# A hybrid decoder trunk on one core: the last feed-forward block and the start of the next layer reordered tile by tile

## What is computed

```python
h = rmsnorm(x, g_pre_mix) * (1 + sc1) + sh1
proj = h @ w_in                  # q, k, v, gates and indexer, 7240 columns
mixed = sigmoid(ga) * moba_attention(...) + sigmoid(gb) * dsa_attention(...)
x = x + gt1 * rmsnorm(mixed @ w_out, g_post_mix)

h = rmsnorm(x, g_pre_ffn) * (1 + sc2) + sh2
f = (silu(h @ w_gate) * (h @ w_up)) @ w_down      # 2816 wide
x = x + gt2 * rmsnorm(f, g_post_ffn)
```

## Time and profile before

| | |
|---|---|
| time, median of 3 runs | 891.76 us (891.47 to 892.01) |
| time of the profiled execution | 891.98 us |
| its span, first to last instruction | 890.1 us |
| TensorE busy with matmuls | 867.8 us, 97% |
| VectorE busy | 660.2 us, 74% |
| ScalarE busy | 411.6 us, 46% |
| GpSimd busy | 133.0 us, 15% |
| mean granted TensorE clock | 0.997 |

### The profile page before, as it was taken

The page is one execution under the profiler, slowest core; times in us unless marked ns, Lnnn a source line. Parts: engine busy times, 40 slices in busy tenths (PEclk is TensorE's granted clock), DMA queues, the critical chain, the costliest instruction groups (busy, mean ns, idle before and its releaser), DMA issues.

```text
span 890.1 us, 11600 instructions
## 1 busy us (share of the span) xinstructions
PE 867.8 (97%) x4241; PEld 713.6 (80%) x4241; DVE 660.2 (74%) x1090; ACT 411.6 (46%) x607; POOL 133.0 (15%) x164
## 2 busy tenths in 40 slices
PE   7999999999999999999999999999999999999996
PEld 5787788888877788888878778888888788888885
DVE  3778999887878767667568899988787865654842
ACT  1264654655636354344336555555564534434421
POOL 6500300200312030110232030020031200000302
PEclk9999999999999999999999999999999999999998
DMA  9787665567442977676634756566744274564611
GB/s 333 298 300 299 214 243 207 216 237 256 143 166 72 361 276 292 246 289 251 235 142 146 292 223 237 214 236 237 244 158 166 73 302 170 219 260 182 209 52 47
DMA packets 35577, 194.61 MB, mean 219 GB/s; under 512 B 4544, under 2 KB 4544, under 8 KB 19008
## 3 DMA queue, kind: packets, MB, share of 16 engines
q1 hardware_dynamic: 33984, 189.62, 57.8%
q0 software_dynamic: 1536, 4.24, 1.5%
HBM read 192.80 MB, written 1.05 MB: 218 GB/s over the span
## 4 chain that ended last, share of the span: by engine, by line
PE 80%; issue 9%; DVE 8%; DMA 2%; POOL 1%; ACT 1%; SPq 0%; DVEq 0%; POOLq 0%; ACTq 0%
PE ps L1142 23%; PE ps L1144 23%; PE ps L1143 23%; PE ps L1196 4%; PE ps L1248 1%; PE ps L1296 1%; DMA raw<-w_ada 1%; DVE pj L983 1%; DVE ffn_m L848 1%; PE ps L1276 1%; DVE x L1006 1%; DVE pj L968 1%; PE ps L1269 1%; PE ps L1268 1%; PE ps L1247 1%
## 5 line engine op out<-in xcount | busy, mean ns | idle before, releaser
L803 DVE TENSOR_TENSOR w_lo<-raw,w_hi 128x2048 fp32r<-128x2048 f32 (+1 forms) x132 | 302.2, 2298 | 52.2 <-ACT w_hi L581 50.3
L1142 PE MATMUL ps<-w_hi,t_hi 128*128 128x512 f32 (+2 forms) x832 | 325.3, 391 | 2.3 <-DVE t_lo L951 1.6
L1144 PE MATMUL ps<-w_hi,t_lo 128*128 128x512 f32 (+2 forms) x832 | 318.7, 383 | 0.0
L1143 PE MATMUL ps<-w_lo,t_hi 128*128 128x512 f32 (+2 forms) x832 | 318.1, 382 | 0.0
L581 ACT ACTIVATE w_hi<-raw 128x2048 fp32r<-128x2048 f32 (+1 forms) x132 | 249.8, 1896 | 25.4 <-DMA raw<-w_stream 16.0
L1142 PEld LDWEIGHTS ps<-w_hi,t_hi 128*128 128x128 f32 x832 | 156.3, 188 | 35.1 <-DVE t_lo L951 3.1
L1144 PEld LDWEIGHTS ps<-w_hi,t_lo 128*128 128x128 f32 x832 | 156.3, 188 | 30.9
L1143 PEld LDWEIGHTS ps<-w_lo,t_hi 128*128 128x128 f32 x832 | 156.5, 188 | 28.6
L1142 PE MATMUL ps<-w_hi,m_hi 128*128 128x512 f32 x240 | 99.6, 415 | 0.3
L1144 PE MATMUL ps<-w_hi,m_lo 128*128 128x512 f32 x240 | 94.3, 393 | 0.0
L1143 PE MATMUL ps<-w_lo,m_hi 128*128 128x512 f32 x240 | 93.7, 390 | 0.0
(11 more groups left out here) (170 smaller groups left out, 898.6 us busy)
## 6 DMA issues: line engine op xcount, KB each, us to landing
raw<-w_stream SPq DMA_DIRECT2D x128, 1024.0 KB, 5.9
ada<-w_ada SPq DMA_DIRECT2D x84, 512.0 KB, 5.0
raw<-w_ada SPq DMA_DIRECT2D x6, 512.0 KB, 11.8
raw<-w_stream SPq DMA_DIRECT2D x4, 656.0 KB, 8.6
scale_t<-gains POOLq DMA_DIRECT2D x4, 512.0 KB, 4.4
gate_t<-gains POOLq DMA_DIRECT2D x4, 512.0 KB, 5.1
pj<-w_ada SPq DMA_DIRECT2D x3, 512.0 KB, 16.1
mixed<-w_ada SPq DMA_DIRECT2D x2, 512.0 KB, 12.5
```

What stands on the lines that cost most here:

```text
L803: nc.vector.tensor_tensor(w_lo[:, U % RING, 0:n], raw[:, U % RAW, 0:n], w_hi[:, U % RING, 0:n].bitcast(F32), ALU.subtract).then_inc(s_lo, 1)
L1142: nc.tensor.matmul(dst, hi, w_h, start=first, stop=False)
L1143: nc.tensor.matmul(dst, hi, w_l, start=False, stop=False)
L1144: return nc.tensor.matmul(dst, lo, w_h, start=False, stop=last)
```

## The change

1. Block 10, the last of the feed-forward part, goes tile by tile on TensorE: up(10), down(9) with `turn_m` between its two banks, down(10), first for tile 0 and then for tile 1. ScalarE and VectorE get a `last_block` each, in which their part of block 10, the norm steps of the border and the splits of the next layer's units 1 to 4 are interleaved.
2. In layer 1 the first three chunks go tile by tile: chunks 0, 1 and 2 of tile 0, with the transposes of tile 1 after seven of the eight steps of chunk 2; then the three chunks of tile 1; then `turn_index`. The first index products move into chunk 3.
3. y is squared and gated in halves, one for each PSUM bank, and TensorE signals each bank. The two sums of a row are added in the first step of the inverse root.
4. VectorE makes all inverse roots of the feed-forward border, and behind the mixer all but that of y of tile 1. Its Newton steps are scalar_tensor_tensor instead of tensor_scalar.
5. h of tile 1 lies in hbuf 2 instead of hbuf 1, so that `copy_chunk` doesn't wait for the transposes of h; the squares' unused output goes to `mixed`.
6. 4 fills instead of 23 behind the feed-forward part.

The diff, cut to its core:

```diff
-MIXER_FILL, FFN_FILL, TURN_FILL = 16, 23, 4
+MIXER_FILL, FFN_FILL, TURN_FILL = 16, 4, 4
...
-OWN_NORMS = [n for n, (l, _, of, t) in enumerate(NORMS) if l >= 0 and of == "x"]
+OWN_NORMS = [n for n, (l, mid, of, t) in enumerate(NORMS)
+             if l >= 0 and (of == "x" or t == 0 or not mid)]
...
-            link(engine.tensor_scalar(u, ssq[:, t:t + 1], EPS, 0.5, ALU.add, ALU.mult))
+            if of == "y":
+                link(engine.tensor_scalar(u, ssq[:, t, 0:1], ssq[:, t, 1:2], EPS / 2, ALU.add, ALU.add))
+            else:
+                link(engine.tensor_scalar(u, ssq[:, t, 0:1], EPS / 2, None, ALU.add))
             link(engine.tensor_scalar(y.bitcast(I32), u.bitcast(I32), -0.5, RSQRT_BITS, ALU.mult, ALU.add))
             for step in range(NEWTON):
-                link(engine.tensor_scalar(e, y, u, y, ALU.mult, ALU.mult))
-                ins = engine.tensor_scalar(y, e, 1.5, y, ALU.subtract, ALU.mult)
+                if engine is nc.vector:
+                    link(engine.scalar_tensor_tensor(out=e, in0=y, scalar=u, in1=y, op0=ALU.mult, op1=ALU.mult))
+                    ins = engine.scalar_tensor_tensor(out=y, in0=e, scalar=1.5, in1=y, op0=ALU.subtract, op1=ALU.mult)
+                else:
+                    link(engine.tensor_scalar(e, y, u, y, ALU.mult, ALU.mult))
+                    ins = engine.tensor_scalar(y, e, 1.5, y, ALU.subtract, ALU.mult)
...
+                if of == "x":
+                    nc.scalar.activation(dst, x[:, t, :], ACT.Square, scale=(2.0 * D) ** -0.5,
+                                         accum_out=ssq[:, t, 0:1]).then_inc(s_sq, 1)
+                    return
+                for half in range(2):
+                    act.wait_ge(s_y, y_no(l, mid, t, half))
+                    nc.scalar.activation(dst[:, 512 * half:512 * half + 512], ps[:, 2 * t + half, :], ACT.Square,
+                                         scale=(2.0 * D) ** -0.5, accum_out=ssq[:, t, half:half + 1]).then_inc(s_sq, 1)
...
+            def last_block(l):
+
+                j, more = N_FF - 1, l + 1 < DEPTH
+                ahead, behind = up_splits(j)
+                split_hi(l, ahead[0])
+                silu(l, j, 0)
+                m_hi_split(l, j, 0)
+                sum_squares(NORMS.index((l, False, "y", 0)))
+                split_hi(l, behind[0])
+                if more:
+                    sum_squares(NORMS.index((l, False, "x", 0)))
+                silu(l, j, 1)
+                m_hi_split(l, j, 1)
+                split_hi(l, behind[1])
+                if more:
+                    h_hi(l + 1, "h1", 0)
+                sum_squares(NORMS.index((l, False, "y", 1)))
+                if more:
+                    split_hi(l + 1, RING - 2)
+                    split_hi(l + 1, RING - 1)
+                    copy_chunk(l + 1, 0, 0)
+                    sum_squares(NORMS.index((l, False, "x", 1)))
+                    copy_chunk(l + 1, 1, 0)
+                    h_hi(l + 1, "h1", 1)
+                    copy_chunk(l + 1, 2, 0)
...
+            def own_rstd(l, mid, of, t):
+
+                n = NORMS.index((l, mid, of, t))
+                dve.wait_ge(s_sq, squares(n))
+                inverse_rms(nc.vector, link, n, s_own_rstd)
...
+                for half in range(2):
+                    cols = slice(512 * half, 512 * half + 512)
+                    dve.wait_ge(s_sq, squares(NORMS.index((l, mid, "y", t)), half))
+                    nc.vector.tensor_tensor(hbuf[:, 2 * t, cols], ps[:, 2 * t + half, :], gate_t[:, cols],
+                                            ALU.mult).then_inc(s_dve, 1)
+                    links[0] += 1
...
+            def middle(l):
+
+                gated(l, True, 0)
+                own_rstd(l, True, "y", 0)
+                added(l, True, 0)
...
+                normed(l, True, 0)
+                gated(l, True, 1)
+                h_lo(l, "h2", 0)
+                added(l, True, 1)
+                scaled(1)
...
+            def last_block(l):
+
+                j, more = N_FF - 1, l + 1 < DEPTH
+                ahead, behind = up_splits(j)
+                split_lo(l, ahead[0])
+                gate_up(l, j, 0)
+                m_lo_split(l, j, 0)
+                gated(l, False, 0)
+                own_rstd(l, False, "y", 0)
+                added(l, False, 0)
                 if more:
-                    dve.wait_ge(s_table, 2 + 4 * l + (2 if mid else 4))
+                    dve.wait_ge(s_table, 2 + 4 * l + 4)
                     scaled(0)
-                    dve.wait_ge(s_shift, 2 * l + (1 if mid else 2))
-                    normed(l, mid, 0)
-                gated(l, mid, 1)
+                gate_up(l, j, 1)
                 if more:
-                    h_lo(to, kind, 0)
-                added(l, mid, 1)
+                    own_rstd(l, False, "x", 0)
+                m_lo_split(l, j, 1)
+                if more:
+                    dve.wait_ge(s_shift, 2 * l + 2)
+                    normed(l, False, 0)
+                    split_lo(l, behind[0])
+                    h_lo(l + 1, "h1", 0)
+                    split_lo(l, behind[1])
+                gated(l, False, 1)
+                own_rstd(l, False, "y", 1)
+                added(l, False, 1)
                 if more:
                     scaled(1)
-                    normed(l, mid, 1)
-                    h_lo(to, kind, 1)
+                    split_lo(l + 1, RING - 2)
+                    own_rstd(l, False, "x", 1)
+                    normed(l, False, 1)
+                    split_lo(l + 1, RING - 1)
+                    h_lo(l + 1, "h1", 1)
```

and on TensorE:

```diff
                 project(l, 0, 0)
-                project(l, 1, 0, lambda: turn_h(l, "h1", 1))
+                if l:
+                    project(l, 1, 0)
+                    project(l, 2, 0, lambda: turn_h(l, "h1", 1), KT - 2)
+                else:
+                    project(l, 1, 0, lambda: turn_h(l, "h1", 1))
                 project(l, 0, 1)
                 project(l, 1, 1)
                 for s in range(2, N_CHUNK + 2):
-                    if s < N_CHUNK:
+                    if s == 2:
+                        project(l, 2, 1 if l else 0)
+                    elif s == 3 and l:
+                        project(l, s, 0, lambda: index_logits(l, 0))
+                    elif s < N_CHUNK:
                         project(l, s, 0)
...
                     if s == 2:
                         turn_index(l)
+                        if l:
+                            continue
...
-                for j in range(1, N_FF):
+                for j in range(1, N_FF - 1):
...
                     turn_m(l, j, 1)
-                    if j < N_FF - 1:
-                        down_chunk(l, j - 1, 1)
-
-                down_chunk(l, N_FF - 1, 0)
-                for j in (N_FF - 2, N_FF - 1):
-                    down_chunk(l, j, 1)
+                    down_chunk(l, j - 1, 1)
+                for t in range(TT):
+                    up(l, N_FF - 1, t)
+                    down_chunk(l, N_FF - 2, t, lambda: turn_m(l, N_FF - 1, t))
+                    down_chunk(l, N_FF - 1, t)
```

More of the change, by code:

```diff
@@ L137, with squares @@
     (l, mid, of, t) for mid in (True, False) for t in range(TT) for of in ("yx" if mid or l + 1 < DEPTH else "y"))]
-OWN_NORMS = [n for n, (l, _, of, t) in enumerate(NORMS) if l >= 0 and of == "x"]
+OWN_NORMS = [n for n, (l, mid, of, t) in enumerate(NORMS)
+             if l >= 0 and (of == "x" or t == 0 or not mid)]
 POOL_NORMS = [n for n in range(len(NORMS)) if n not in OWN_NORMS]
+def squares(n, half=1):
+    return sum(2 if of == "y" else 1 for _, _, of, _ in NORMS[:n]) + (half + 1 if NORMS[n][2] == "y" else 1)
 def last_norm(n):
@@ L418, in _ @@
             for l in range(DEPTH):
-                for u in range(RAW, RING):
+                for u in range(RING - 2 if l else RAW, RING):
                     load_unit(l, u)
@@ L565, in _ @@
                     finish_shift(n + 5, 2 * l + 2)
-                for i in range(6 + 8 * l, min(10 + 8 * l, len(NORMS))):
-                    norm(i)
         @block.scalar
@@ L758, in _ @@
                         rectify(l, 2 * (s - 3) + 1)
-                    if s < N_CHUNK:
+                    if s < N_CHUNK and (s > 2 or l == 0):
                         copy_chunk(l, s, 0)
-                border(l, True)
-                for j in range(N_FF):
+                middle(l)
+                for j in range(N_FF - 1):
                     ahead, behind = up_splits(j)
@@ L782, in _ @@
                     split_hi(l, behind[1])
-                border(l, False)
+                last_block(l)
         @block.vector
@@ L1010, in _, with middle @@
             made = [0, 0]
-            def border(l, mid):
-                to, kind = (l, "h2") if mid else (l + 1, "h1")
-                more = to < DEPTH
-                gated(l, mid, 0)
-                added(l, mid, 0)
+            def middle(l):
+                gated(l, True, 0)
+                own_rstd(l, True, "y", 0)
+                added(l, True, 0)
```

(13 more changed lines are left out.)

137 lines of the change are left out of this document (62 added, 75 removed).

## The result

The changed kernel takes 894.46 us (median of 7 runs, 893.44 to 895.17), the kernel before 891.76 us (median of 7, 891.47 to 892.17). The ratio is 1.0027 with a 95% interval of 1.0018 to 1.0036: slower by a little more than can be told from no change. I had forecast 891.8 us, and 890.0 to 893.5 us for the case that my sum held. The profiled execution of the changed kernel took 893.93 us with a span of 892.1 us, 1.95 us more than the profiled 891.98 us of before, and 0.5 us under its own median.

What follows compares the result with a forecast made beforehand. TensorE held 80% of the chain of waits, and the layer border was a serial chain over VectorE. Border 2.1, middles -1.0 and end -1.1 summed to 0.0, so 891.8 us, range 889.2 to 895.3.

Steps and rivals of the forecast that it cites:

- my sum: Whole kernel: 2.1 - 1.0 - 1.1 = 0.0 us of change, hence 891.8 us; chance 0.50, within 890.0 to 893.5.
- An unchanged layer 0 start adds nothing: Start of layer 0: no change in time; copy_chunk loses a wait, but its consumers there come later anyway.
- rival 1: Layer 1's projection 2: TensorE's half clock outlasts its cover, 2 to 4 us more, 895; chance 0.22.
- Rival 2: VectorE's norm chain is longer, steps nearer 0.35 than 0.22 us, 3.9 us more, 895.7; chance 0.11.
- Border: Layer 0 to layer 1: projection 0 starts 4.8 us earlier, but turn_qk of chunk 2 comes 2.1 us later.
- the rope of chunk 2: Before turn_qk of chunk 2 in layer 1: TensorE waits 0.9 us more for VectorE's rope.
- The clock: Layer 1's projection 2: clock falls to 1.2 GHz within the 4.0 us wait, hidden by the wait for unit 4.
- The middles: Two middle borders: 0.5 to 0.6 us won at each, -1.0 us together, bounds 0 to -1.4.
- The end: End of the kernel: tile 1's y no earlier, but half squares, half gates and VectorE's norm give -1.1 us.
- rival 4: VectorE's chain is shorter, norms at 1.5 us, no wait for rope: 889.2 us; chance 0.14.
- Rival 3: Border: projections cover tile 1's norm, VectorE needing under 10 us to unit 4, not 16.4: 884.3 us; chance 0.03.
- Rival 5: The change acts only at end and middle, the border coming out even: 889.7 us; chance counted with rival 4.

Runs made afterwards that it cites:

- the one with the pad: The changed kernel plus 48 unused one-column operations at the end of GpSimd's program; 891.36 us, ratio 0.9999.
- the ninth kernel: The changed kernel plus 48 unused operations ending GpSimd's program, with one Newton step instead of three in layer 0's four border norms; 889.4 us, ratio 0.9969.
- the fills: The changed kernel plus 16 dummy 512-column matmuls between chunks 1 and 2 of tile 0 in layer 1; 895.24 us, ratio 1.0037.
- the twelfth kernel: The seventh kernel with layer 1's last block also in the order of the kernel before, halves and VectorE norms kept; 888.0 us, ratio 0.9953.
- seventh: The changed kernel with layer 0's border in the order before, three of its norms on VectorE, 40 unused operations ending GpSimd's program; 888.15 us, ratio 0.9958.

## Why the prediction came out as it did

**The step that failed** is the sentence "An unchanged layer 0 start adds nothing". I had looked there for changed waits and found one that was lost. That the start could move without a changed instruction was not among the rivals. In place of nothing, GpSimd stood idle for 10.39 us behind its first cast, and the start measured +3.01 us in the profiled execution, and 3.1 us between the medians of the changed kernel and of the one with the pad, 891.36, which lies 0.4 us from my 891.8 us. That 894.46 us still lies within my outer range, 889.2 to 895.3 us, is luck: the range was opened upwards for rivals 1 and 2, and neither of them came.

**Border, +2.1 forecast, +1.85 measured.** The unit costs held: norms of 1.8 and 1.7 us, steps of 0.22 and 0.16, VectorE without a gap for 16.3 us (16.4), waits of 3.78 (4.0) and 0.66 us (2.6 at full rate; see the clock). Projection 0 starts 5.2 us earlier after the first silu of block 10 (4.8). The wait for the rope of chunk 2 is 0.55 us (0.9). That the border loses although a wait of 2.74 us on GpSimd went fits what the prediction names: units 1 and 2 can only be split once tile 1's last up products have freed their places, so tile by tile puts both into VectorE's chain. That this chain is the bound is shown by the ninth kernel. The old border shows the price of the order as a whole, 1.85 + 1.44 = 3.3 us; the two splits alone were not tried.

**The clock.** The fall in the first wait came, and was hidden, as forecast: without it the second wait would have been 2.2 us (the fills' 2.15). Against rival 1, the clock did come back: from 476.5 on the products are 0.23 us apart again, before the critical ones. That was partly luck: with the fills the same seven slow products cost 1.46 us, and in the kernel with 48 operations of pad, behind the same wait of 3.78 us, all twelve products of the first half are 0.43 us apart (granted clock 0.50 from 470 to 475), so that the second half starts 0.15 us after its split is done and its first product is slow too.

**The middles, -1.0 forecast, -1.45 measured.** The mechanism was right; the term was too small, at 0.5 us for each, where the second tile's first product moved by 0.71. The 0.65 us by VectorE's path were near; what made 0.5 of them was that TensorE would be ready only 0.2 us before its turn, and it still waited 0.75 us there, as before. **The end, -1.1, measured -1.13.** That tile 1's y would come no earlier by the new order is shown by the twelfth kernel.

**Not in the sum:** -0.33 us over layer 0's feed-forward, in steps of 0.04 us a block. It appears in most of the kernels, not in the one with 16 fills, nor from the fifth block on in the twelfth, and not in layer 1. Its cause is open.

**Rival 2** (dearer norms) and **rival 4** (cheaper ones) fell with the 1.8 us. **Rival 3** needed VectorE under 10 us; it had 16.3. **Rival 5** (the border even) fell with the border's 1.85 us. The five known terms without the start come to 1.85 - 1.45 - 1.13 - 0.33 = -1.06 us; in their profiled executions the kernel with 24 operations of pad has -1.01 and the one with 48 has -0.48.

## What to carry to other kernels

When a measured time is off by a few microseconds, compare the start of the same operation in both traces all along the kernel, before looking at the place that was changed: the loss may stand where the diff has no line. Before tiles are put one behind the other to overlap a serial step, list what their last product frees, since loads and splits that wait for that place move onto the chain too. Before a fill is put in front of one wait, look whether a second wait follows ahead of the critical work: here it did, and the slow products only moved behind it.

## What the runs showed that I had not expected

GpSimd stood idle for 10.2 to 11.5 us behind its first cast (10.24, 10.35, 10.39, 10.77, 10.77, 11.31, 11.51) in all seven kernels whose GpSimd program has 100 to 124 operations in the page, and 0.34 or 0.35 us in all seven with 140 or 164, the kernel before among them. Operations added to the end of the program close the gap at the start; as many on TensorE do not. In the six kernels with a pad an idle time of 10.9 to 11.3 us stands in front of the pad instead. Single small operations of GpSimd that take 1.0 to 1.4 us instead of 0.2 to 0.3 stand in the first 36 us of all fourteen kernels, gap or not; one of 2.98 us (at 40.88 in the changed kernel) stands in the five kernels with the gap that make the input's norms on GpSimd, and in none without it. The price of the gap is 3.1 us in the changed kernel and 3.65 in the one with the old border (891.8 less 888.15; 3.5 when each is compared with its own runs of before). The releaser is "issue", and between the start of the span and 24 us no packet of an instruction queue was recorded in either of the two kernels, before and changed, so the cause behind the length is not shown; whether it is the length itself, or the place in memory that follows from it, stays open. The Trainium skill, page "Runtime: NRT & Kernel Launch", section "Instruction fetch mechanics", says that an engine's instructions come in blocks of 256 and that the cost of going from one block to the next is mostly hidden. The first half would fit a boundary between 124 and 140 operations, most of which have a wait of their own beside them; it fits less well that the idle time in front of the pad stays at the pad's first operation when the program has eight operations more ahead of it (the seventh and twelfth kernels). If the idle time were such a fetch, the second half would not hold at this place, by 10 us. No run here shows the fetch. Another trail is in the trace's record of GpSimd's sequencer, which the views leave out: its last instruction ahead of the idle time is a MODIFY_POOL_CONFIG, at 8.62 us in the changed kernel and at 833.87 us, ahead of the pad, in the kernel with 48 operations of pad; in the latter the same instruction at the start, at 9.38 us, is followed by work after 0.1 us. What it has to do with the idle time was not tried.

A one-column scalar_tensor_tensor on VectorE takes 0.22 us with one pointer and 0.16 us without, as drawn from the slope of the earlier trace rows.
